# Last down projection with the tokens' side standing in TensorE and the weights moving 512 wide

## The reference

```
mix = concatenate([yc, ya], axis=-1) @ w_out
x = x + rms_norm(mix, post_mix_g)
h = rms_norm(x, pre_mlp_g)
f = square(relu(h @ w_up)) @ w_down          # w_up 2048 x 8192, w_down 8192 x 2048
x = x + rms_norm(f, post_mlp_g)              # the norm divides by the root mean square of a token's 2048 values
return x
```

## Time and profile before

| | |
|---|---|
| median of three runs | 2807.31 us (2805.01 to 2810.2) |
| the profiled execution's own time | 2804.35 us |
| its span, first to last instruction | 2802.6 us |
| TensorE busy | 2708.7 us, 97% of the span |
| VectorE, ScalarE, GpSimd busy | 1973.3, 1330.2, 162.1 us |
| mean granted TensorE clock | 0.992 |
| chain that ended last | TensorE 84%, VectorE 7%, DMA 4% |

### The profile page before, as it was taken

One profiled execution on the slowest core, in us unless ns is written; L12 is line 12 of the kernel. 1 busy time (PEld: TensorE's weight loads), 2 busy tenths in 40 slices (PEclk: granted clock), 3 DMA queues, 4 the chain that ended last, 5 costly groups with the idle time before them and its releaser, 6 DMA issues.

```text
span 2802.6 us, 42463 instructions
## 1 busy us (share of the span) xinstructions
PE 2708.7 (97%) x16744; PEld 2418.4 (86%) x16744; DVE 1973.3 (70%) x3083; ACT 1330.2 (47%) x2117; POOL 162.1 (6%) x146
## 2 busy tenths in 40 slices
PE   8989999999999999999999999999999999999997
PEld 7778888888899788888888889998888888888886
DVE  6778667777896886555555679997667566575665
ACT  2165453334444544444444554467554444444454
POOL 0000000000002000000000170111100000000001
PEclk9999999999999999999999999999999999999999
DMA  9944245567887686555555555543535555555553
GB/s 385 397 145 167 84 153 194 198 215 244 318 308 249 231 300 203 190 188 188 188 189 193 186 169 174 177 168 130 179 130 189 191 189 190 189 188 189 188 188 128
DMA packets 158455, 565.27 MB, mean 202 GB/s; under 512 B 17584, under 2 KB 21936, under 8 KB 158256
## 3 DMA queue, kind: packets, MB, share of 16 engines
q1 hardware_dynamic: 158256, 562.56, 59.0%
HBM read 560.39 MB, written 2.10 MB: 201 GB/s over the span
## 4 chain that ended last, share of the span: by engine, by line
PE 84%; DVE 7%; DMA 4%; ACT 3%; issue 1%; SPq 0%; POOL 0%; ACTq 0%; DVEq 0%
PE BK L355 21%; PE BK L353 21%; PE BK L356 10%; PE BK L352 10%; PE BK L358 5%; PE BK L360 4%; PE BK L359 4%; PE BK L445 2%; DVE LO L690 2%; DMA RAW<-wst_dram 1%; ACT HI L538 1%; PE BK L364 1%; DMA EARLY<-wst_dram 1%; DMA RAW<-wada_dram 1%; DVE RAW L678 1%
## 5 line engine op out<-in xcount | busy, mean ns | idle before, releaser
L538 ACT ACTIVATE HI<-RAW 128x1024 fp32r<-128x1024 f32 x826 | 875.9, 1061 | 1189.5 <-PE BK L353 816.0
L690 DVE TENSOR_TENSOR LO<-RAW,HI 128x1024 fp32r<-128x1024 f32 x826 | 1012.7, 1227 | 370.4 <-ACT HI L538 370.0
L355 PE MATMUL BK<-H,HI 128*128 128x512 f32 x2672 | 1070.3, 402 | 11.9 <-DVE LO L690 11.5
L353 PE MATMUL BK<-H,HI 128*128 128x512 f32 x2640 | 1042.4, 396 | 0.0
L356 PE MATMUL BK<-H,LO 128*128 128x256 f32 x2672 | 743.2, 278 | 0.0
L352 PE MATMUL BK<-H,LO 128*128 128x256 f32 x2640 | 738.2, 280 | 0.4 <-DVE H L728 0.2
L352 PEld LDWEIGHTS BK<-H,LO 128*128 128x128 f32 x2640 | 496.9, 188 | 118.1 <-DVE H L728 2.0
L356 PEld LDWEIGHTS BK<-H,LO 128*128 128x128 f32 x2672 | 504.2, 189 | 106.5 <-issue 0.7
L355 PEld LDWEIGHTS BK<-H,HI 128*128 128x128 f32 x2672 | 508.6, 190 | 23.8 <-DVE LO L690 15.1
L353 PEld LDWEIGHTS BK<-H,HI 128*128 128x128 f32 x2640 | 496.2, 188 | 3.8
L358 PE MATMUL BK<-H,HI 128*128 128x256 f32 x1296 | 382.3, 295 | 13.2 <-DVE LO L690 7.2
(11 more groups left out here) (249 smaller groups left out, 2035.7 us busy)
## 6 DMA issues: line engine op xcount, KB each, us to landing
RAW<-wst_dram SPq DMA_DIRECT2D x840, 512.0 KB, 3.3
RAW<-wada_dram SPq DMA_DIRECT2D x154, 512.0 KB, 4.8
EARLY<-wada_dram SPq DMA_DIRECT2D x38, 512.0 KB, 12.3
EARLY<-wst_dram SPq DMA_DIRECT2D x18, 512.0 KB, 13.9
X<-xT_dram SPq DMA_DIRECT2D x8, 512.0 KB, 6.9
B<-bias_dram SPq DMA_DIRECT2D x32, 128.0 KB, 3.3
out_dram<-X SPq DMA_DIRECT2D x3, 512.0 KB, 2.6
CN<-consts_dram SPq DMA_DIRECT2D x1, 900.0 KB, 14.6
```

What stands on the lines that cost most here:

```text
L353: e.matmul(bk[:, :], hh, H[:, k, :], start=False, stop=last, skip_group_check=True).then_inc(S["tile"], 1)
L355: e.matmul(bk[:, :], hh, H[:, k, :], start=first, stop=False, skip_group_check=True)
L538: e.activation(HI[:, u % NHL, :], raw_at(slot), ACT.Copy).then_inc(S["hi"], 1)
L690: e.tensor_tensor(LO[:, u % NHL, :], raw_at(slot), HI[:, u % NHL, :].bitcast(f32), sub).then_inc(S["lo"], 1)
```

## The change

The last w_down is computed token-major. The activations H2[:, k, 128 tokens] stand, and four neighbouring weight tiles of one k, HI and LO of half a unit, move as 512 columns. For each k and each group g of 512 output features there are two halves m of the tokens, and three matmuls for each. Sixteen k fill two banks, one for each m. The sums come out as YT[128 tokens, m, 2048 features]. So a token's squares are a row sum, taken by ScalarE with its accumulating output, in place of squares, GpSimd adds and a product against ones. The norm's weight now varies along the free dimension; a DMA spreads it over all partitions at the start of this feed-forward. X, which is still feature-major, is turned by 32 TensorE transposes at the end, and the output is stored token-major.

```diff
+            def load_gain(free):
+                q.wait_ge(free)
+                e.dma_start(GAIN, gain_d.rearrange("(a n) -> a n", a=1).broadcast_to([128, 2048])).then_inc(S["gain"], 16)
...
+            def tile_tokens(u, i, bks, H, k, first, last, lo, h, free, at):
+                q.wait_ge(lo, h, free)
+                hh = HI[:, u % NHL, i * 128:i * 128 + 512]
+                ll = LO[:, u % NHL, i * 128:i * 128 + 512]
+                for m in range(2):
+                    e.matmul(bks[m][:, :], H[:, k, 128 * m:128 * m + 128], hh, start=first, stop=False, skip_group_check=True)
+                    e.matmul(bks[m][:, :], H[:, k, 128 * m:128 * m + 128], ll, start=False, stop=False, skip_group_check=True)
+                    r = e.matmul(bks[m][:, :], H[:, k, 256 + 128 * m:384 + 128 * m], hh, start=False, stop=last, skip_group_check=True)
+                r.then_inc(S["tile"], 4)
+
+            def x_turn(bk, m, g, ready, free):
+                q.wait_ge(ready, free)
+                for n in range(4):
+                    r = e.transpose(bk[:, 128 * n:128 * n + 128], X[:, 4 * g + n, 128 * m:128 * m + 128], cn("ident"))
+                r.then_inc(S["at_p"], 1)
...
+            def square_sum(c, src, ready):
+                q.wait_ge(ready)
+                e.activation(SQT[c], src, ACT.Square, accum_out=SUMT[:, c:c + 1]).then_inc(S["st_a"], 1)
...
+            def total(ready):
+                q.wait_ge(ready)
+                e.tensor_reduce(VT, SUMT.rearrange("p (m g) -> p m g", m=2), AX, add).then_inc(S["st_v"], 1)
...
-            def evd2(ci, j):
-                if ci < 3:
-                    return ev_y(ci, j)
-
+            gain_tok = load("load_gain", "gain", y_end)
+            t_tok = {(m, g): None for m in range(2) for g in range(4)}
+
+            def ev_tokens(ci, g, m):
                 def f(bk, tok, own):
-                    if j == 15:
-                        spin(3)
-                        y_tok[j] = combine(Y[j], bk, Y[j], add, tok, own, y_tok[j])
+                    if not ci and not y_free:
+                        y_free.extend(now())
+                    dst = YT[:, m, 512 * g:512 * g + 512]
+                    if ci == 0:
+                        t_tok[m, g] = do("copy_sum", "ev_a", dst, bk[:, :], tok, y_free)
                     else:
-                        yield from ev_y(ci, j)(bk, tok, own)
-                    ST.square(Y[j], y_tok[j], final=(j == 15))
-                    y_tok[j] = do("gained", "ev_a", Y[j], Y[j], col("post_mlp", j), ST.sq)
+                        t_tok[m, g] = do("tensors", "ev_v", dst, bk[:, :], dst, add, tok, t_tok[m, g])
+                    own[0].release(own[1], t_tok[m, g])
+                    if ci == 3:
+                        sq_tok[m, g] = do("square_sum", "st_a", 4 * m + g, dst, [t_tok[m, g], *rx_used])
+                        yield
+                        t_tok[m, g] = do("tensors", "ev_v", dst, dst, GAIN[:, 512 * g:512 * g + 512], mult, [sq_tok[m, g], gain_tok])
                     yield
                 return f
-            ffn((16, 16, 16, 16), up2, first2, "w_down2", evd2, lambda ci, j: (ci, j) != (3, 15))
-            rs_tok = ST.finish(2048, 1e-6, now())
-
-            for a, b in LAST_ROWS:
-                rb = RS[:, 0, :].unsqueeze(1).broadcast_to([128, b - a, 256])
-                k = do("tensors", "ev_v", rows_of(B2, a, b), rows_of(B2, a, b), rb, mult, [rs_tok] + y_tok[a:b])
-                k = do("tensors", "ev_v", rows_of(X, a, b), rows_of(X, a, b), rows_of(B2, a, b), add, [k] + x_tok[a:b])
-                load("store", "out", a, b, k)
...
+                for k in range(16):
+                    u, i = divmod(w.tile, 8)
+                    w.tile += 4
...
+                    tok = do("tile_tokens", "tile", u, i, bks, H2, k, k == 0, k == 15, lo_tok[u], need(f_tok, k), frs if k == 0 else None, n=4)
+                    if k == 15:
+                        for m in range(2):
+                            later(ev_tokens(ci, g, m)(bks[m], tok, own[m]), EVLAG if (ci, g) != (3, 3) else 0)
...
+            turned = {}
+            for g in range(4):
+                for m in range(2):
...
+                    ring = lbank if lbank.idle else mbank
+                    bi, bk, fr = ring.get()
+                    turned[m, g] = bk, do("x_turn", "at_p", bk, m, g, x_tok[4 * g + 3], fr)
+            w.run_pending()
+            k = do("total", "st_v", [sq_tok[m, g] for m in range(2) for g in range(4)])
+            r = whole(rsqrt_steps(NT, HT, VT, 1.0 / 2048, 1e-6, k))
+            for m in range(2):
+                for a in range(2):
+                    for g in (2 * a, 2 * a + 1):
+                        dst = YT[:, m, 512 * g:512 * g + 512]
+                        bk, tk = turned[m, g]
+                        k = do("scaled", "ev_v", dst, dst, NT[:, m:m + 1], bk[:, :], mult, add, [r, tk], t_tok[m, g])
+                    load("store", "out", m, 1024 * a, k)
```

More of the change, by code:

```diff
@@ L198, with program @@
            "at_v", "at_g", "cv_a", "cv_v", "cv_p", "spin")
-LOADS = tuple(f"raw{i}" for i in range(NRAW + NEARLY)) + tuple(f"bias{i}" for i in range(4)) + ("cols", "consts", "x0", "x1", "x2", "x3", "pos", "xr", "out")
-def program(nc, xT, pos, cols_d, consts_d, wada, wst, bias_d, out, log):
+LOADS = tuple(f"raw{i}" for i in range(NRAW + NEARLY)) + tuple(f"bias{i}" for i in range(4)) + ("cols", "consts", "x0", "x1", "x2", "x3", "pos", "xr", "gain", "out")
+def program(nc, xT, pos, cols_d, consts_d, wada, wst, bias_d, gain_d, out, log):
     f32 = mybir.dt.float32
@@ L294, in program @@
         YA = [B2[:, i, :] for i in range(16)]
+        YT = B2[:, 0:16, :].rearrange("p a t -> p (a t)").rearrange("p (m n) -> p m n", m=2)
+        GAIN = B1[:, 0:8, :].rearrange("p a t -> p (a t)")
+        SQT = [pair(B1, 8 + 2 * i) for i in range(8)]
+        SUMT, VT, NT, HT = SM[:, 0:8], SM[:, 8:10], SM[:, 10:12], SM[:, 12:14]
         GB = [GBT[:, i, :] for i in range(16)]
@@ L334, in load_bias, with store @@
                 e.dma_start(BB[i % 4], bias_d[i]).then_inc(S[f"bias{i % 4}"], 16)
-            def store(a, b, ready):
+            def load_gain(free):
+                q.wait_ge(free)
+                e.dma_start(GAIN, gain_d.rearrange("(a n) -> a n", a=1).broadcast_to([128, 2048])).then_inc(S["gain"], 16)
+            def store(m, a, ready):
                 q.wait_ge(ready)
-                e.dma_start(out[:, a:b, :], X[:, a:b, :]).then_inc(S["out"], 16)
+                e.dma_start(out[:, m, a:a + 1024], YT[:, m, a:a + 1024]).then_inc(S["out"], 16)
             walk(dict(load_cols=load_cols, load_consts=load_consts, load_x=load_x, load_x2=load_x2, load_pos=load_pos,
-                      load_ada=load_ada, load_unit=load_unit, load_bias=load_bias, store=store), log)
-            e.wait_ge(S["out"], 16 * len(LAST_ROWS))
+                      load_ada=load_ada, load_unit=load_unit, load_bias=load_bias, load_gain=load_gain, store=store), log)
+            e.wait_ge(S["out"], 16 * N_STORES)
         def tensor(e):
@@ L513, in conv_square_sum @@
                 r.then_inc(S["cv_p"], 1)
-            walk(dict(tile=tile, direct=direct, c_spread=c_spread, spin=spin, stat_add=stat_add, stat_sum=stat_sum, acc2_sum=acc2_sum, rope_turn=rope_turn, ba_turn=ba_turn,
+            walk(dict(tile=tile, tile_tokens=tile_tokens, x_turn=x_turn, direct=direct, c_spread=c_spread, spin=spin, stat_add=stat_add, stat_sum=stat_sum, acc2_sum=acc2_sum, rope_turn=rope_turn, ba_turn=ba_turn,
                       cumulate=cumulate, row_sum=row_sum, spread=spread, g_spread=g_spread, g_heads=g_heads, g_turn=g_turn,
@@ L917, in vector @@
                       split_lo=split_lo, tensors=tensors, scaled=scaled, root_half=root_half, root_out=root_out,
-                      stat_product=stat_product, gain=gain, normed=normed, rope_cos=rope_cos, rope_halves=rope_halves, rope_sin=rope_sin, taps=taps,
+                      stat_product=stat_product, total=total, gain=gain, normed=normed, rope_cos=rope_cos, rope_halves=rope_halves, rope_sin=rope_sin, taps=taps,
                       ba_copy=ba_copy, softplus_in=softplus_in, decay_log=decay_log, cumulated=cumulated, beta_gate=beta_gate,
@@ L2370, in f, with tokens @@
                     yield
                 return f
-            ffn((16, 16, 16, 16), up2, first2, "w_down2", evd2, lambda ci, j: (ci, j) != (3, 15))
-            rs_tok = ST.finish(2048, 1e-6, now())
-            for a, b in LAST_ROWS:
-                rb = RS[:, 0, :].unsqueeze(1).broadcast_to([128, b - a, 256])
-                k = do("tensors", "ev_v", rows_of(B2, a, b), rows_of(B2, a, b), rb, mult, [rs_tok] + y_tok[a:b])
-                k = do("tensors", "ev_v", rows_of(X, a, b), rows_of(X, a, b), rows_of(B2, a, b), add, [k] + x_tok[a:b])
-                load("store", "out", a, b, k)
+            def tokens(f_tok, at, ci, g):
+                own, bks, frs = [], [], []
+                for m in range(2):
```

(50 more changed lines are left out.)

4 lines of the change are left out of this document (2 added, 2 removed).

## The result

The changed kernel takes 2792.22 us (2790.4 to 2793.81, four runs) against 2808.69 (2805.01 to 2810.2, four runs). The ratio is 0.9947, with a 95% interval from 0.9934 to 0.9959, or -14.9 us (-11.5 to -18.5).

The account below looks back on a forecast made before the run. The prediction took TensorE's matmul pitch to bound the body and VectorE's chain the tail; -3.6 us in the tail and -0.2 in the matmuls made -3.8, from 2807.3 to 2803.5 us, range 2796 to 2809.5.

Parts of the forecast that it names:

- What bounds the kernel: Last down projection bound by TensorE's matmul pitch with no wait left; the 17.5 us tail set by VectorE's chain.
- TensorE's part: Last down projection: pitch goes with the columns, 1536 matmuls at 232.3 ns, 356.8 us, -0.2 us.
- The sign that I named for being wrong: Last down projection: the prediction is wrong if a 512-column matmul's pitch depends on its neighbours; no size given.
- Rival 1: Last down projection: each matmul has a fixed cost, 10.3 ns, so fewer save 5.3 us; 2798.2 us, chance 0.22.
- Rivals 2 and 3: Last down projection: all-512 streams reach 217 ns, 2779.5 us, chance 0.06; or are slower than the mixed one, chance 0.06.
- No wait at the chunks' starts: Last down projection: TensorE busy 89.05 of 89.10 us in the last chunk, so no wait left to remove.
- The tail: From VectorE's start on the last bank to the end: 14.0 us instead of 17.5, -3.6 us.
- The root: In the tail: the norm's root ready 4.7 us after VectorE starts on the last bank, table load setting the pace.
- the end after the last `scaled`: In the tail: the last store, 512 KB instead of 256, ends 3.1 us after the last scaling operation.
- The eight `scaled`: In the tail: eight VectorE scalings of 128x512 at 0.775 us each with the gap, 6.2 us.
- The transposes: In the tail: turning X takes TensorE 0.89 us a bank, 7.1 us for eight, hidden with 0.8 us to spare.
- Evictions, gain row: Last down projection: emptying banks and loading the norm's weight cost nothing, covered by idle time of engines and DMA.

Follow-up runs that it names:

- e1: Changed kernel with the LO product issued as two 256-column matmuls, giving widths 512, 256, 256, 512; 2802.47 us, a down chunk 89.18 us.
- e2: Kernel before, with LO also meeting all 512 columns of H in the last down projection; a down chunk took 116.06 us.
- e4: Changed kernel with every 512-column matmul issued as two of 256; 1.0019 of the time before, a down chunk 92.16 us.
- e7: Kernel before, with the first two blocks of each last down chunk side by side; 2807.98 us, a chunk 89.22 us instead of 89.51.
- e6: Changed kernel with each of the tail's 32 transposes made three times; the tail took 15.56 us, 2.5 more.
- e8: Changed kernel with ScalarE's table loaded earlier, the total before the last gain product and the last store cut in two; 0.9943 of the time before.
- e11: Repeat of the changed kernel with early table load, earlier total and last store cut in two; 0.9944 of the time before.

## Why the prediction was wrong

- **What bounds the kernel**: right for the body, where no wait of note was left. In the tail it is VectorE's chain up to the first store; from there the stores fill the DMA engines and go at the same pace as VectorE, which the prediction didn't see.
- **TensorE's part: this is the step that failed.** I wrote that the pitch goes with the columns, gave two thirds of a period to its two 512s, and so took 232.3 ns for each of them and -0.2 us for the whole projection. The start of a matmul in such a stream doesn't show what it costs by itself: e1 has the same starts with operands whose 512 takes 226.7 in its own company, and e2 has 226.7 with the old operands. Only the length of a whole period holds. 1536 matmuls at 226.7 are 348.2 us, where I had 356.8. The sign that I named for being wrong, that the pitch of a 512 depends on its neighbours, came near it: the distance between two starts depends on them, the cost of a whole period only by 3.3 ns.
- **Rival 1 was the mechanism**, and I gave it 0.22. I priced a matmul at 10.3 ns from the narrow and the wide tile, and half a matmul fewer for each tile at -5.2 ns. It is 13.3 ns by e2 and e4 together, and the mixed stream pays another 3.3 for each period of four (e1), which hid a part of the cost when I took narrow less wide. A tile falls from 348.4 to 340.0, -8.4 ns, 8.6 us over 1024. What spoke against the rival, the 0.11 for a 256, was the same misleading reading. Rivals 2 and 3 are out by the same number: 226.7 is neither 217 nor above 235. The time still lies 6.0 us below the 2798.2 of rival 1, so its mechanism was right and its price too small.
- **No wait at the chunks' starts**: the claim that there was none to remove was wrong by 1.2 us, shown by e7. The busy share of a stretch, 89.05 of 89.10, is too coarse for 0.3 us.
- **The tail**: -4.5 against -3.6. The root came out as worked, and so did the end after the last `scaled`, though in part by luck: it holds because the stores, which fill the DMA engines, keep pace with VectorE. The eight `scaled` have a pitch of 0.67 us where I had 0.775 from the 256-wide rows, 0.8 us in all. The transposes were hidden, as I wrote, but on a misread row: line 445, which I took for transposes, is in `g_pair`, plain fp32 products with two records each, 0.22 us. A transpose is one record, with a pitch of 0.118 us in the tail (3.79/32). At three times their length, in e6, two `scaled` wait 2.4 us together; at the single one none waits.
- **Evictions, gain row**: at nothing, as forecast. The only waits for LO in the second feed-forward are two near its start, 2.5 us in all, and both kernels have them.
- **The sum**: 2803.5 forecast, 2792.2 measured. Of the 11.3 us between them the pitch explains 8.6, the H2 waits 1.2 and the tail 0.9; the 0.6 left is within the scatter of the medians.

## What to carry to other kernels

Count the matmuls as well as the columns. In fp32r a matmul cost 1/2.4 ns for each column and some 13 ns beside them here, so the form with the wider moving operand won, though not a column was saved. To price a new form from an old trace, use the lengths of whole periods of different widths, and don't take a pitch from the starts of two neighbours of a mixed stream. A difference of two such periods isn't enough by itself: narrow less wide gave 10.3 ns. With 1/2.4 ns a column, which e2 and e4 give, 768 columns are 320 ns; the wide tile's 348.5 then leave 28.5 for two matmuls and the narrow tile's 358.8 leave 38.8 for three, 14.2 and 12.9 each, on both sides of the 13.3 that was measured. In a tail, look at the DMA engines' share as well as at the chain: where they were full, a smaller last store brought nothing (e8). Where the last accumulated rows are the last to arrive, an order that wants them late hid their wait here.

## What the runs showed of the hardware

- The cost beside the columns is 13.3 ns for a matmul in fp32r (226.7 ns at 512 columns, 120.0 at 256) and 2.1 in bf16 (215.4 at 512). A 512, 256, 256, 512 period in fp32r takes 3.3 ns more than these add up to (696.7 against 693.4).
- Letting 64 and 128 columns stand by turns made three matmuls 8 ns slower, though the loads got shorter.
- fp32 transposes of 128x128 take 0.118 us each in the changed kernel's tail and 0.111 in e6, and in e6 they held TensorE's clock at 2.4 GHz for 10.6 us with nothing else on the engine.
- Output stores issued 1.3 us apart fill the 16 DMA engines at some 395 GB/s; a 256 KB store at their end lands after 2.7 us (e8, e11), against 2.0 where the engines had pauses between stores (the kernel before).
